# A hybrid decoder layer on one core: the order of eight head pairs, and where a gated-delta pair's convolutions are made

## The reference

```
h = rms_norm(x, norm_w);  proj = h @ w_in          # 2048 -> 8204 columns
o_ret = retention(rq, rk * 128**-0.5, rv)          # chunks of 128
y_ret = rms_norm(o_ret, ret_norm_w) * silu(rg)
qkv   = silu(causal_depthwise_conv(gqkv, conv_w))  # 4 taps, gated-delta only
gq, gk = l2_norm(gq) * 128**-0.5, l2_norm(gk)
beta  = sigmoid(gb);  g = -exp(a_log) * softplus(ga + dt_bias)
o_gdn = gated_delta_rule(gq, gk, gv, g, beta)      # chunks of 64, a triangular solve per chunk
y_gdn = rms_norm(o_gdn, gdn_norm_w) * silu(gz)
y_moba = softmax_attention(rms_norm(mq), rms_norm(mk), mv) * silu(mz)   # one block of 256, ALiBi
out = x + concat(y_ret, y_gdn, y_moba) @ w_out
```

## Time and profile before

| | |
|---|---|
| median of 3 runs | 569.23 us (566.64 to 569.46) |
| the profiled execution | 565.8 us, span 564.0 us |
| PE busy | 545.4 us, 97% of the span |
| DVE, ACT, POOL busy | 334.4, 280.9, 95.7 us |
| gated-delta pairs' windows, 68 to 264 us | PE busy 192.1 of 196 us |
| retention pairs' windows, 264 to 362 us | PE busy 97.7 of 98 us |

### The profile page before, as it was taken

How to read it: one execution, slowest core, us unless ns; L and a number is a source line. 1 busy time by engine, 2 the same in 40 slices (tenths; PEclk the granted TensorE clock), 3 DMA queues, 4 the chain that set the end, 5 groups by cost and what they waited for, 6 DMA issues and landing times.

```text
span 564.0 us, 8809 instructions
## 1 busy us (share of the span) xinstructions
PE 545.4 (97%) x3446; PEld 465.9 (83%) x3446; DVE 334.4 (59%) x525; ACT 280.9 (50%) x450; POOL 95.7 (17%) x95
## 2 busy tenths in 40 slices
PE   5799999999999989999999999999999999999997
PEld 4687888887888878888988888888888888888885
DVE  2875876767678596545374446475457446655451
ACT  3655663455444653446644555465446446533340
POOL 2102120213121130112121112132131212000000
PEclk9799999998999999999999999999999999999999
DMA  9895564545245554555469648656765666487711
GB/s 292 212 299 130 149 180 119 149 115 148 78 113 139 138 135 113 150 150 130 131 166 234 160 114 233 180 147 163 201 160 142 190 192 187 143 280 218 237 56 37
DMA packets 149788, 91.80 MB, mean 163 GB/s; under 512 B 7828, under 2 KB 139123, under 8 KB 149491
## 3 DMA queue, kind: packets, MB, share of 16 engines
q1 hardware_dynamic: 148562, 89.14, 58.3%
q10 hardware_dynamic: 1184, 2.11, 1.0%
HBM read 89.13 MB, written 2.10 MB: 162 GB/s over the span
## 4 chain that ended last, share of the span: by engine, by line
PE 92%; DVE 4%; ACT 2%; DMA 1%; issue 0%; SPq 0%; ACTq 0%
PE pj L1115 39%; PE pj L1116 19%; PE pj L1136 5%; PE pj L1137 5%; PE pj L1134 5%; PE pj L1112 2%; PE mx L1257 2%; PE mx L1247 2%; PE pj L1111 1%; PE mx L1234 1%; DVE w_lo L278 1%; PE mx L1224 1%; DMA cst<-table_dram 1%; PE mx L1189 1%; PE pj L1158 1%; ACT w_hi L359 1%
## 5 line engine op out<-in xcount | busy, mean ns | idle before, releaser
L1115 PE MATMUL pj<-hT,w_hi 128*128 128x512 f32 x960 | 354.3, 407 | 3.5 <-DVE th L738 2.3
L1116 PE MATMUL pj<-hT,w_lo 128*128 128x256 f32 x960 | 270.1, 281 | 0.0
L278 DVE TENSOR_TENSOR w_lo<-w_raw,w_hi 128x1024 fp32r<-128x1024 f32 x158 | 198.2, 1262 | 109.4 <-ACT w_hi L359 108.9
L359 ACT ACTIVATE w_hi<-w_raw 128x1024 fp32r<-128x1024 f32 x160 | 168.1, 1054 | 104.3 <-PE pj L1116 66.6
L1115 PEld LDWEIGHTS pj<-hT,w_hi 128*128 128x128 f32 x960 | 182.0, 190 | 44.2 <-DVE th L738 2.6
L1116 PEld LDWEIGHTS pj<-hT,w_lo 128*128 128x128 f32 x960 | 183.0, 191 | 2.4
L647 POOL TENSOR_TENSOR raw<-ev 128x256 f32<-128x256 f32 x64 | 57.9, 906 | 316.5 <-ACT ev L367 316.4
L367 ACT ACTIVATE ev<-pj 128x512 f32<-128x512 f32 x64 | 37.9, 594 | 70.3 <-PE pj L1112 69.2
L1134 PE MATMUL pj<-w_hi,yT 128*128 128x512 f32 x128 | 50.3, 393 | 0.0
L1137 PE MATMUL pj<-w_lo,yT 128*128 128x512 f32 x128 | 49.9, 390 | 0.0
L1136 PE MATMUL pj<-w_hi,yT 128*128 128x512 f32 x128 | 49.8, 389 | 0.0
(11 more groups left out here) (211 smaller groups left out, 416.6 us busy)
## 6 DMA issues: line engine op xcount, KB each, us to landing
w_raw<-in_w_in_dram SPq DMA_DIRECT2D x256, 256.0 KB, 3.4
w_raw<-in_w_out_dram SPq DMA_DIRECT2D x64, 256.0 KB, 3.5
w_raw<-in_x_dram SPq DMA_DIRECT2D x2, 1024.0 KB, 6.0
cv<-in_x_dram SPq DMA_DIRECT2D x8, 256.0 KB, 5.1
out_dram<-sq ACTq DMA_DIRECT2D x8, 256.0 KB, 4.6
cst<-table_dram SPq DMA_DIRECT2D x1, 676.0 KB, 5.9
cst<-table_dram SPq DMA_DIRECT2D x1, 196.0 KB, 5.0
dd<-in_w_in_dram SPq DMA_DIRECT2D x1, 96.0 KB, 5.7
```

The costliest lines, as they stand in the source:

```text
L278: eng.tensor_tensor(w_lo[:, n % NSPLIT, :], w_raw[:, n % NRAW, :], w_hi[:, n % NSPLIT, :].bitcast(F32), ALU.subtract).then_inc(S(name), 1)
L359: act.activation(w_hi[:, n % NSPLIT, :], w_raw[:, n % NRAW, :], ACT.Copy).then_inc(S("hi_done"), 1)
L1115: pe.matmul(pj[s][:, :], high, hT[:, kc].rearrange("p a t -> p (a t)"), start=first, stop=False)
L1116: ins = pe.matmul(pj[s][:, 0:T], low, hT[:, kc, 0, :], start=False, stop=False)
```

## The change

`PAIRS` alternates gated-delta and retention pairs. What prepares gdn 1 and gdn 2 leaves `mix_gdn` and is made at the end of `mix_ret`, which now lies in front of each of them. `decay_rows` stands at offset 50 there. The waits on semaphores follow the new order. Each pair's own steps, the constants of the offsets, and all operations with their shapes stay.

```diff
-PAIRS = [("gdn", 0), ("gdn", 1), ("gdn", 2), ("ret", 0), ("ret", 1), ("moba", 0), ("moba", 1), ("moba", 2)]
+PAIRS = [("gdn", 0), ("ret", 0), ("gdn", 1), ("ret", 1), ("gdn", 2), ("moba", 0), ("moba", 1), ("moba", 2)]
...
-U_RET = {"gram": -6, "s1": 2, "qs": 10, "o": 10, "tr": 30}
+U_RET = {"gram": -6, "s1": 2, "qs": 10, "o": 10, "tr": 30, "decay": 50}
...
 ACT, mix_gdn
-                if more:
-                    advance(U["y4"])
-                    tanh_kq(j + 1, 0)
...
-                if more:
-                    decay_exp(j + 1)
...
                 squares(p)
-                if more:
-                    square_first(j + 1)
-                    advance(base + 109)
-                    tanh_kq(j + 1, 1)
-                    square_second(j + 1)
 ACT, end of mix_ret
+                advance(base + 48)
+                tanh_kq(j + 1, 0)
+                advance(U["decay"] + 5)
+                decay_exp(j + 1)
+                square_first(j + 1)
+                advance(base + 109)
+                tanh_kq(j + 1, 1)
+                square_second(j + 1)
...
 DVE, mix_gdn
-                    elif l == 3 and more:
-                        conv(j + 1, 0, 0)
-                    elif l == 4 and more:
-                        conv(j + 1, 0, 1)
...
-                            if more:
-                                decay_clip(j + 1)
-                                conv(j + 1, 0, 2)
...
-                        if more:
-                            decay_mask(j + 1)
...
-                if more:
-                    conv(j + 1, 1, 0)
                 advance(base + 85)
...
-                if more:
-                    silu_kq(j + 1, 0)
                 advance(base + 93)
                 mean_square(p, True)
-                if more:
-                    conv(j + 1, 1, 1)
                 advance(base + 101)
                 norm_out(p, True)
-                if more:
-                    silu_kq(j + 1, 1)
                 advance(base + 109)
 DVE, end of mix_ret
+                conv(j + 1, 0, 0)
+                advance(base + 41)
+                conv(j + 1, 0, 1)
+                advance(base + 53)
+                decay_clip(j + 1)
+                silu_kq(j + 1, 0)
+                advance(base + 61)
+                conv(j + 1, 0, 2)
+                decay_mask(j + 1)
+                advance(base + 93)
+                conv(j + 1, 1, 0)
+                advance(base + 101)
+                conv(j + 1, 1, 1)
+                advance(base + 109)
+                silu_kq(j + 1, 1)
...
 PE, mix_gdn
-                if j == 0:
-                    pe.wait_ge(S("clip_done"), 4)
+                pe.wait_ge(S("clip_done"), 4 * j + 4)
...
-                    if l == 4 and j + 1 < GDN // 2:
-                        pe.wait_ge(S("g_norm"), j + 1)
-                        decay_rows(j + 1)
...
-                pe.wait_ge(S("clip_done"), 4 * min(j + 2, GDN // 2))
 PE, end of mix_ret
+                stream(U["decay"])
+                pe.wait_ge(S("os_full"), p + 1)
+                decay_rows(j + 1)
```

More of the change, by code:

```diff
@@ L395, in advance @@
                         g, s = finished(v - TAP_AFTER)
-                        if 0 < g < GDN and s < 3:
+                        if g and PAIRS[g // 2][0] == "gdn" and s < 3:
                             first_tap(g, s)
@@ L481, in mix_gdn @@
                 U = {k: base + v for k, v in U_GDN.items()}
-                more = j + 1 < GDN // 2
                 advance(U["ktr"] - 4)
@@ L836, in mean_square @@
                     dve.tensor_tensor(sm[:, 104:108], sm[:, 48:52], sm[:, 112:116], ALU.mult).then_inc(S("o_ms0"), 1)
-                    dve.wait_ge(S("o_ms0"), p + 1)
+                    dve.wait_ge(S("o_ms0"), PAIRS[p][1] + 1)
                     dve.tensor_scalar(sm[:, 52:56], sm[:, 104:108], EPS, None, ALU.add).then_inc(S("o_ms"), 1)
@@ L1143, in block_ready @@
             def block_ready(b):
-                order = {"ret": 3, "gdn": 0, "moba": 5}
-                kind = "ret" if b < 2 else "gdn" if b < 5 else "moba"
-                p = order[kind] + b - {"ret": 0, "gdn": 2, "moba": 5}[kind]
+                kind, first = ("ret", 0) if b < 2 else ("gdn", 2) if b < 5 else ("moba", 5)
+                p = PAIRS.index((kind, b - first))
                 pe.wait_ge(S("y_lo"), p + 1)
```

## The result

| | before | changed |
|---|---|---|
| median | 569.20 us (566.64 to 569.46, 4 runs) | 562.52 us (562.08 to 563.26, 4 runs) |
| ratio, 95% interval | | 0.9894 (0.9863 to 0.9925) |
| profiled execution | 565.8 us, span 564.0, mean clock 0.991 | 562.88 us, span 561.1, mean clock 0.994 |
| PE busy | 545.4 us | 542.9 us |

The change is 1.1% faster: 6.7 us between the medians, but only 2.9 us between the two profiled executions. The forecast was 565.4, within 562.4 to 568.4, for a saving of 3.8 us; the measured 562.52 lies 0.1 us above the lower end.

What follows compares the result with a forecast made beforehand. PE, 97% busy, was taken as the bound, so only its waits and clock could give: 4.1 + 1.6 us gone, 1.9 us new, 3.8 us saved from the 569.2 us median, giving 565.4 us, range 562.4 to 568.4.

Steps and rivals of the forecast that it cites:

- The bound: PE busy 97% of the span; waits of 4.1 us and clock loss of 1.6 us, at most 5.7 us removable.
- The end of gdn 0: Transposes' wait for the normed output falls from 1.08 us to 0.3, bounds 0 and 0.6, as the factor meets POOL's add.
- `decay_rows`, at cost 0 in all: Four transposes moved inside PE's stream, issued either way: cost 0.
- The start of ret 0: New PE wait of 1.0 us at the first retention gram, for DVE's `yf` behind one more `w_lo`.
- The ends of gdn 1 and gdn 2: Each waits 0.31 us at its transposes, bounds 0 and 0.6, in place of 2.67 and 0.31.
- The retention pairs at cost 0: Retention pairs take 11.2 us more DVE and some 5 us more ACT work in free time, costing PE nothing.
- The deadline's spare time: Preparation at a retention pair's end is ready about 1 us before the next gated-delta gram.
- The clock behind the first border: Behind gdn 0 the slow-clock stretch, priced at 1.6 us, goes.
- the last of the sum: The profiled execution's 3.8 us saving, 565.8 to 562.0, applied to the 569.2 median, giving 565.4 us.
- The term for the 2.67 us wait: At the end of gdn 1, PE's idle 2.67 us counted as wait alone, with the clock at 1.00 around it.
- rival 4: More is gained: factor misses the add, two later pairs don't wait; saved 4.7 us, time 564.5; chance 0.14.
- Rival 1: Clock falls at border 0's new wait too, price 1.6 us again: saved 2.2, time 567.0; chance 0.15.

Runs made afterwards that it cites:

- the best group: Executions of the unchanged kernel before at mean clock 0.991, the fastest of its groups: 566.06 to 567.10 us, middle 566.5.
- the trace that caught it: The kernel before, unchanged, profiled again: 568.86 us at mean clock 0.988, with a second half-clock stretch behind gdn 1.
- the kernel at 561.49 us: Changed kernel with, in retention pairs, ACT's decay exponential and square behind unit 65 instead of 55, DVE's mask behind 77: 561.49 us, ratio 0.9901 against the kernel before.

## Why the prediction was right, and where it was short

*The bound*: right for the profiled execution, where PE's waits at one line and the clock behind the first were 5.7 us. For the median it left out a fall of 3.3 us behind gdn 1.

*The end of gdn 0*: right in size and cause. 0.3 us was taken between 0 and 0.6, and 0.32 was measured; the factor met POOL's add and ended with it. The middle of two bounds was a choice, so that it came out to 0.02 us is luck: POOL's add started at 132.19, not 132.9, and PE was at the transposes at 133.97, not 134.5. `decay_rows`, at cost 0 in all, no longer lay in that stretch. Of the port lock that the Trainium skill states (SBUF — State Buffer, who interferes with whom) this trace shows the effect a second time, though the wait came out in the middle, since the add lasted 1.30 us and started under a `w_lo` of DVE.

*The start of ret 0*: right, 1.01 us for 1.0, with `yf` behind one `w_lo` on DVE.

*The ends of gdn 1 and gdn 2*: right, 0.3 us each.

*The retention pairs at cost 0*: wrong by 0.5 to 0.6 us. The free time on each engine was counted, but not the order in it: ACT stands at `decay_exp` for DVE's clips, and DVE's mask comes before a `w_lo` that is due. The run that moved ACT's exponential and DVE's mask shows that this cost was real (two waits of 0.3 and 0.2 us) and avoidable; which of the two moves did it is open. The deadline's spare time, "about 1 us", measured 0.86.

*The clock behind the first border*: right as a gain of 1.6 us, and the rival that it would fall again at the new wait did not come: 1.00 in its window.

*The step that was short* is the last of the sum: "the same saving gives 565.4 us". It put the profiled execution's waits and clock on the median. That execution had a clock of 0.991 and belonged to the best group; by its time the median of 569.2 stood for executions whose clock fell behind gdn 1 as well. The term for the 2.67 us wait was 2.67 us; in these executions it is that plus a fall, which cost 3.3 us in the trace that caught it. The sign was there to see: the median lay 3.4 us above the profiled execution, and that difference was carried over unexplained.

Two errors then met. From 565.4 the fall takes 3.3, which leaves 562.1, and the saving between profiled executions was 0.9 us smaller than forecast, which gives 563.0, against 562.5 measured. The lower end of the range was made from rival 4 and the scatter of runs (564.5 less 2 is 562.5, written as 562.4), not from this fall. That the measured time lies just inside is luck.

Rival 1 took from the Trainium skill (TensorE: Matmul & The Clock Gate, HAM oscillation) that idle gaps between bursts of matmuls put the clock down. The gaps of that section are longer than any wait here, so by its rule neither border would have fallen; here the clock fell behind 1.08 us in all four profiles with the first wait unfilled and the old order of steps, and behind 2.67 us in some. The rival was weighed for the new wait only, and it was the old one that it bore on.

Between the profiled executions, 2.9 us were measured for 3.8 forecast: 0.6 are the waits for `w_lo`, and about 0.15 is the start, since the first gram begins at 73.80 us in place of 73.65; the remaining 0.15 was not traced.

## What to carry to other kernels

Where one engine is full, a wait in it costs its length and, in some executions, the slow clock behind it as well. So look at the mean clock of every execution, not of the profiled one alone: if times fall in groups, one profile shows one group, and its windows, not the mean alone, say where the clock was lost. A step put behind another engine's result delays everything queued on its own engine; give it the units by which that result is late, as in the kernel at 561.49 us.

## What the hardware showed that I had not expected

The same program with the same 2.67 us wait kept its full clock behind it in some executions (1.00 from 202 to 206 us) and fell to half in another (0.50), which cost 3.3 us. Transposes of a constant in PE's idle time, which serve nothing, made the kernel before 0.55% faster (ratio 0.9945). Waits of 2.8 us at two borders brought 574.8 us, where waits of 0.55 us brought 564.6: 10.3 us for 4.4 us of waiting.
